# 24 table loads per head pair issued by SyncE in one step instead of in four: a three-block sequence kernel on one core

## The reference, cut to what matters

```python
h = jnp.einsum('btd,de->bte', x, w_in) + b_in
q_a, k_a, v_a, g_a, q_h, z_fwd, z_bwd, i_h, g_h = jnp.split(h, split_at, axis=-1)
o_a = neighbourhood_attention(heads_a(q_a), heads_a(k_a), heads_a(v_a), rpb)
# inside it, for each block of 16 query columns and 32 key columns:
bias = rpb[:, dr[:, None, :, None], dc[None, :, None, :]]
s = jnp.where(in_win[...], s + bias[None].astype(jnp.float32), -jnp.inf)
```

## Time and profile before

| | us |
|---|---|
| median of 3 runs | 4429.78 |
| lowest and highest | 4420.64, 4433.94 |
| the profiled execution | 4429.78 |
| its span | 4428.0 |
| TensorE busy | 4208.6 (95%) |
| VectorE, ScalarE, GpSimd busy | 2680.5, 1798.1, 662.0 |

### The profile page before, as it was taken

One profiled execution on the slowest core, in us unless ns is written; L12 is line 12 of the kernel. 1 busy time (PEld: TensorE's weight loads), 2 busy tenths in 40 slices (PEclk: granted clock), 3 DMA queues, 4 the chain that ended last, 5 costly groups with the idle time before them and its releaser, 6 DMA issues. The chain is left out here.

```text
span 4428.0 us, 62175 instructions
## 1 busy us (share of the span) xinstructions
PE 4208.6 (95%) x24346; PEld 3427.4 (77%) x24346; DVE 2680.5 (61%) x4238; ACT 1798.1 (41%) x3434; POOL 662.0 (15%) x308
## 2 busy tenths in 40 slices
PE   6999999999999999999989989999899999999689
PEld 5888888889888877788767768888787787777467
DVE  6788888872566642144467667566456546466465
ACT  5111111111466641122466646555446446355553
POOL 2111111110333221011011112332000000000111
PEclk9999999999999999999999989999899999999799
DMA  5111111122544431211389882588666466556553
GB/s 184 43 53 53 53 53 53 53 67 84 187 135 128 129 127 38 69 56 69 139 277 294 273 299 104 172 273 285 208 211 199 160 204 205 178 183 198 196 183 123
DMA packets 515499, 663.94 MB, mean 150 GB/s; under 512 B 60476, under 2 KB 407424, under 8 KB 491786
## 3 DMA queue, kind: packets, MB, share of 16 engines
q1 hardware_dynamic: 466778, 577.13, 40.0%
q10 hardware_dynamic: 48432, 82.85, 5.0%
HBM read 442.24 MB, written 217.65 MB: 149 GB/s over the span
## 5 line engine op out<-in xcount | busy, mean ns | idle before, releaser
L229 PE MATMUL ps<-hh,wsplit 128*128 128x512 f32 x2048 | 817.9, 399 | 4.7 <-DVE hl L953 3.7
L230 PE MATMUL ps<-hl,wsplit 128*128 128x512 f32 x2048 | 814.2, 398 | 0.0
L231 PE MATMUL ps<-hh,wsplit 128*128 128x512 f32 x2048 | 808.8, 395 | 0.0
L982 DVE SCALAR_TENSOR_TENSOR conv_acc<-conv_in,pcol,conv_acc 128x1024 f32<-128x1024 f32 x480 | 687.9, 1433 | 14.8
L229 PEld LDWEIGHTS ps<-hh,wsplit 128*128 128x128 f32 x2048 | 387.0, 189 | 104.0 <-issue 8.0
L230 PEld LDWEIGHTS ps<-hl,wsplit 128*128 128x128 f32 x2048 | 389.9, 190 | 93.8 <-issue 4.3
L231 PEld LDWEIGHTS ps<-hh,wsplit 128*128 128x128 f32 x2048 | 385.8, 188 | 88.0
L221 POOL TENSOR_TENSOR wsplit<-wraw,wsplit 128x1024 fp32r<-128x1024 f32 x72 | 200.9, 2801 | 1338.9 <-ACT wsplit L216 1338.9
L3804 PE MATMUL ps<-h_hi,w 128*128 128x512 f32 x896 | 378.1, 422 | 7.9 <-DVE h_lo L3063 4.4
L3805 PE MATMUL ps<-h_lo,w 128*128 128x512 f32 x896 | 357.1, 399 | 0.0
L3806 PE MATMUL ps<-h_hi,w 128*128 128x512 f32 x896 | 356.7, 398 | 0.0
(11 more groups left out here) (427 smaller groups left out, 8753.8 us busy)
## 6 DMA issues: line engine op xcount, KB each, us to landing
w<-w_split_tiles SPq DMA_DIRECT2D x108, 1024.0 KB, 5.4
wraw<-in_w_in SPq DMA_DIRECT2D x72, 512.0 KB, 3.9
w_split_tiles<-w SPq DMA_DIRECT2D x36, 1024.0 KB, 6.9
sh<-hy_ak ACTq DMA_DIRECT2D x48, 512.0 KB, 4.1
g_tiles<-b_ost SPq DMA_DIRECT2D x80, 256.0 KB, 5.0
w_raw<-in_w_in SPq DMA_DIRECT2D x36, 512.0 KB, 4.7
wo_raw<-in_w_out SPq DMA_DIRECT2D x32, 512.0 KB, 6.5
sh<-hy_ad ACTq DMA_DIRECT2D x32, 512.0 KB, 8.4
```

The costliest lines, as they stand in the source:

```text
L229: e.matmul(p[:, :], wh, c.HH[tb][:, k, :], start=k == 0, stop=False)
L230: e.matmul(p[:, :], wh, c.HL[tb][:, k, :], start=False, stop=False)
L231: t = e.matmul(p[:, :], wl, c.HH[tb][:, k, :], start=False, stop=k == 7)
L982: e.scalar_tensor_tensor(v, a[:, h * 1024 + j:(h + 1) * 1024 + j], c.convw(j, ch), v, ALU.mult, ALU.add) \
```

## The change

Before, the 24 loads of a head pair are eight steps of three loads, two steps behind each of positions 4 + 6 pr, 5 + 6 pr, 6 + 6 pr and 7 + 6 pr. After, they are one step of 24 loads behind position 5 + 6 pr. The loads themselves, their order among themselves and the waits ahead of the first one are the same.

```diff
     after(1, "bounds")
     for pr in range(4):
-        for q in range(8):
-            after(4 + 6 * pr + q // 2, "bias_ld", pr, q // 4, q % 4)
+        after(5 + 6 * pr, "bias_ld", pr)
...
-    def bias_ld(pr, h, a):
+    def bias_ld(pr):
+        e.wait_ge(*L.tr[3, 1])
         t = L.BT[:, pr % 2, :].rearrange("p (t i x) -> p t i x", t=3, x=32)
-        if h == 0 and a == 0:
-            e.wait_ge(*L.tr[3, 1])
-            e.wait_ge(*L.rd_st[0])
-            if pr >= 2:
-                e.wait_ge(*L.bd_st[pr % 2][pr - 2, 1])
-        for pat in range(3):
-            src = bass.AP(L.RD.tensor, ((2 * pr + h) * 15 + a) * 128 + 48 - 8 * pat, [[1, 16], [128, 12], [1, 32]])
-            e.dma_start(t[64 * h + 16 * a:64 * h + 16 * a + 16, pat, :, :], src).then_inc(*L.t_ld[pr % 2].up((pr, h, a, pat)))
+        e.wait_ge(*L.rd_st[0])
+        if pr >= 2:
+            e.wait_ge(*L.bd_st[pr % 2][pr - 2, 1])
+        for h in range(2):
+            for a in range(4):
+                for pat in range(3):
+                    src = bass.AP(L.RD.tensor, ((2 * pr + h) * 15 + a) * 128 + 48 - 8 * pat, [[1, 16], [128, 12], [1, 32]])
+                    e.dma_start(t[64 * h + 16 * a:64 * h + 16 * a + 16, pat, :, :], src).then_inc(*L.t_ld[pr % 2].up((pr, h, a, pat)))
```

More of the change, by code:

```diff
@@ L3210, in b3_sp @@
         elif k == "bias_ld":
-            bias_ld(*s[1:])
+            bias_ld(s[1])
         elif k == "bias_st":
```

## The result

The changed kernel takes 4452.92 us (median of 6 runs, 4446.66 to 4456.67) against 4430.11 us (6 runs) before. The ratio is 1.0055, with a 95% interval of 1.0045 to 1.0066: slower by 20 to 29 us. The forecast of 4465 us had the sign and the place right and was 12 us too high.

What follows compares the result with a forecast made beforehand. TensorE, busy 95% of the span, was taken as the bound. Burst and clock delays summed to 31.9 us at position 28, SyncE's lateness to at most 38; the middle, +35 on 4429.8, gave 4465 us, range 4440 to 4484.

Steps and rivals of the forecast that it cites:

- The cover and the place: SyncE's queue, positions 4 to 25: a store's 6.5 us landing wait covers only about a third of a burst.
- Length of one burst: 24 bias loads on SyncE's queue: four times a typical 4.8 us group, 19.2 us, bounds 13.9 and 26.2.
- First burst: Behind position 5: load of tile 10 goes out 13.3 us late, tile 11 delays position 10 by 11.8 us.
- Second burst: Behind position 11: late tile 21 delays position 20 by 4.7 us, plus 2.6 us for the clock.
- Third: Behind position 17: late tile 22 delays position 22 by 2.0 us, plus 2.5 us for the clock.
- Fourth: Behind position 23: late tile 28 delays position 28 by 5.8 us, plus 2.5 us for the clock.
- What would have been a sign of being wrong: Landings shortening once the bias loads are out of the way, or TensorE's waits being for ScalarE's work, not tiles.
- rival B: Between bursts: stores land in 5 us or less, the queue catches up, mainly position 10 loses 10.3 us; 4442 us, chance 0.12.
- Rival C: Late tiles hold ScalarE's recurrence work on in-order engines and bursts may take 26.2 us: +60, 4490 us, chance 0.10.
- rivals D and E: D: buffers hide bursts or they issue in 13.9 us, 4425 to 4430, 0.04; E: landings fall to 3.9, 4412, 0.04.
- The x rows at position 36: Ahead of position 36: SyncE decides, up to 38 us late against TensorE's 31.9, so +35 was taken.
- rival A: The forecast itself: +35 us, own range +22 (landings of 6.0) to +50 (bursts of 22 us), chance 0.70.

Runs made afterwards that it cites:

- Experiment 1: Changed kernel with each burst of 24 bias loads replaced by 8 wider loads, half the bytes, in the same place: 4428.46 us, ratio 0.998.
- Experiment 2: Changed kernel with each of the 24 loads reading 16 pieces of 1536 bytes instead of 192 of 128: 4456.55 us, ratio 1.0045.
- experiment 8: Eight wider loads per head pair, and the second visit's last attention values moved behind position 36, past the x rows: 4426.13 us, ratio 0.998 to the kernel before.
- experiment 9: Changed kernel with the burst of 24 between the weight load and the tile store of its position: 4463.32 us, ratio 1.0064.
- Experiment 4: Changed kernel with ScalarE's rounding of a weight tile moved behind the recurrence's exponentials of the same position: 4457.92 us, ratio 1.005.

## Why the prediction was right, and where a size was off

**The cover and the place: shown.** Experiment 1 keeps the single step and makes it fit into the landing wait, and the loss is gone. Experiment 2 keeps the issues and removes the packets, and the loss stays. It is the number of issues on SyncE's queue.

**The queue sets the length of the stretch: shown by all the profiles.** In twelve of them (all but experiment 8, which moves these loads) position 36 begins 11.0 to 12.2 us after SyncE issues the x rows ahead of it, while the stretch runs from 264.0 to 303.5 us. In the changed kernel these loads are issued 27.4 us later than before, counted from position 4, and position 36 begins 27.2 later. What TensorE waits for on the way, a tile or VectorE, lies inside this.

**Length of one burst: the term that was mis-sized.** The prediction has 19.2 us, four times a group of six. The bursts take 13.3 to 14.6 us. In a group of six before, the issues start 0.47, 1.55, 1.28, 0.53 and 0.48 us apart (the group at 2885.84); in the first burst they start 0.43, 1.59, 1.21 and 0.53 apart, and from there on 0.48, but for one step of 1.62. In experiment 9, where no store stands ahead, there is no such start: 0.58, then 0.48 each. So a store ahead costs some 2 us once, and each further issue 0.48. Multiplying the group by four paid for that start four times. The group of 4.75 and 18 more issues of 0.48 make 13.4. The lower bound of 13.9 was nearly right, for another reason.

**How late the queue was,** by the load of a weight tile, counted from position 4, in us. The column forecast is the prediction's time for the load, less that of before, with its 11.8 us for the first burst added from tile 16 on.

| load of tile | forecast | measured |
|---|---|---|
| 10, behind the first burst | 13.3 | 10.0 |
| 16, behind the second | 25.0 | 17.6 |
| 21 | 21.1 | 16.4 |
| 22, behind the third | 34.2 | 23.7 |
| 27 | 28.5 | 20.8 |
| 28, behind the fourth | 41.7 | 29.9 |

Two errors lie in it and lean against each other: each burst was taken some 5 us too long, and between the bursts the queue was taken to run at 6.9 us per load, which regained more than it did (34.6 us forecast from tile 16 to tile 21, 37.3 measured). Of the measured values 1.3 us were there ahead of the first burst, from a store ahead of it that landed in 8.2 instead of 6.9 us (issued at 2863.86; 2870.83 before).

**First burst:** forecast +11.8, measured +8.6 at position 10. With 14.5 in place of 19.2 the same sum gives 7.1, and the 1.3 us just named make 8.4, so the method holds.

**Second burst:** forecast +4.7 for a tile at position 20 and +2.6 for the clock. Measured +7.4 from position 10 to position 20, but none of it is a wait for a tile: it is 1.24, 1.26, 1.94 and 3.90 us behind VectorE and ScalarE. **Third:** forecast +2.0 for a tile at position 22 and +2.5 for the clock. The wait did not come, and the 1.4 us measured are the clock alone (16.23 us of busy TensorE at 1.00 before, 17.63 at 0.90 after), by the idle time ahead of position 20. **Fourth:** forecast +8.3 with the clock, measured +3.8 to position 28, where the bias wait of 2.51 us is gone, and 6.7 more to position 29. In all the forecast had 31.9 us at position 28; 21.2 were there, 27.9 at position 29 and 28.6 at position 35.

**The clock:** forecast 7.6 us in three places, measured 4.4 in all (7.2 in the second profile), and none of it begins at position 22. That the first burst adds none was right: from position 10 to 20 TensorE was busy 76.2 us before and 75.8 after.

**What would have been a sign of being wrong** came in part. Behind position 10 TensorE's new waits are for VectorE, which ScalarE's work behind a late rounding held up, and not for tiles. The sum for positions 20, 22 and 28 took a path from load to tile to TensorE that did not decide there; that the total still came out near rests on the queue, which is late whatever TensorE waits for. That the second burst came to 7.4 us where 7.3 were forecast is luck. Of the other signs, SyncE's wait at its line 2989 grew to 98 us (106 forecast), and the distance from position 10 to position 36 by 18.6 us (23 forecast).

**The queue catches up, rival B:** refuted. What the queue regained between the bursts is 5 us in all, and the landings kept their median of 6.9 us without bias loads beside them, and the weight loads behind the first burst follow at 6.7 to 7.1 us (behind the second at 6.8 to 8.8). The rule of the Trainium skill that lighter load on HBM shortens the fixed cost (DMA: Bandwidth & Descriptors, "Latency and other measured facts") agrees with the bias loads, which land in 2.3 instead of 4.2 us; the 1 MB stores that set the pace show none of it. No run here tells a lighter load on HBM from a lighter load on the DMA engines.

**Rival C, work held on in-order engines:** half of its mechanism is there (the 8.65 us at ScalarE), its price is not. Experiment 4 shows that it takes the place of the tile wait and does not add to it. The slow burst of 26 us did not come. Of rivals D and E nothing came: the first burst alone makes position 10 late, and the landings of the stores did not shorten.

**The x rows at position 36:** I added 3 us because SyncE would be later than TensorE. The wait there fell from 12.88 to 11.21 us. This step failed: the shorter bursts left SyncE 20 us late with the x rows (3121.30 to 3141.65), which is 27 us counted from position 4, no more than TensorE. That SyncE decides there was right.

**The sum:** +35 forecast, +20 to +29 measured. The weight load behind the first burst is 8.7 us later than the landing alone would make it (15.7 against 6.95 from load to load). Four such excesses are 35 us. The four read from the trace are 8.7, 8.8, 7.3 and 9.1. At the x rows the queue was 27 us late, so it regained 8 in its waits, and TensorE was as late as the queue. One slip in the recorded text: it calls the range that of rival A without its far ends, but 4484 lies above A's own +50, which is 4480.

## What to carry to other kernels

In this kernel an issue on the DMA queue was free only inside a wait that the queue had anyway. Before grouping small transfers into one step, take the gap between the transfers around them, subtract what already stands in it, and compare it with the time of one short group plus the marginal price of each further issue; a group just over the gap already loses (12 issues here), and one just under it is free (8 wider ones). When a late load feeds several engines, the wait of the last one may be booked under another cause, so follow the load and not the label. And look for the place where the critical engine next waits for the queue itself: the lateness there, and not the sum of the waits on the way, is what the change costs.

## What the runs showed of the hardware that was not expected

- Back to back, small transfers start 0.48 us apart with 192 packets of 128 bytes and 0.46 with 16 of 1536. Right behind a 1 MB store two of the first three steps are 1.0 to 1.7 us instead (some 2 us more in all), and now and then a single step of 1.4 to 2.0 us stands in a burst. With no store just ahead 24 of them take as little as 11.6 us.
- With a 512 KB load issued just ahead of a 1 MB store, the store lands in 6.2 to 6.7 us around the first burst, with no small transfer behind it, with six or with 24. When a burst of 12 to 14 us lies between the load and the store (experiment 9), it lands in 4.0 to 5.7 us.
